# Three of four gated FFNs by Strassen's seven products, on one core

## The chip, the cores and the metric

The kernel runs on one core of one Trainium2 chip. The metric is the device time of one execution in microseconds (us); lower is better. Engines are called TensorE (PE), VectorE (DVE), ScalarE (ACT), GpSimd (POOL) and SyncE (SP, which only issues transfers here).

## What is computed

A trunk of two layers on 520 tokens (512 of a prompt and 8 single ones), model width 1024. Each layer has a gated FFN, a mixer, a second gated FFN and an embedding gate:

```
def swiglu(x, wg, wu, wd):
    return (jax.nn.silu(x @ wg) * (x @ wu)) @ wd
...
x = x + 0.5 * swiglu(rms_norm(x, n_ffn1[i]), w_ffn1_gate[i], w_ffn1_up[i], w_ffn1_down[i])
mix, v, new_buf, hT = hybrid_mix(rms_norm(x, n_mix[i]), ...)
x = x + mix
x = x + 0.5 * swiglu(rms_norm(x, n_ffn2[i]), w_ffn2_gate[i], w_ffn2_up[i], w_ffn2_down[i])
gate = jax.nn.sigmoid(rms_norm(x, n_ple[i]) @ w_ple_gate[i])
x = x + gate * (p @ w_ple_proj[i])
```

The FFN's hidden width is 2816, which is 22 tiles of 128. All data are float32.

## The kernel before

Activations lie feature-major: 128 partitions by 8 feature tiles (XT) by 520 tokens (TOK), and a token row is worked on in two halves of 260 (HALF). Every matrix product is done three times in a rounded format: each operand is cut into a high part (the value rounded to float32r) and a low part (the rest), and the products high by high, high by low and low by high add up in PSUM. So one 128x128 block of weights against 520 tokens is 6 matmuls of 260 columns, and a unit of 8 blocks (one output tile of 1024 inputs) is 48.

Weights come as a stream of units of 512 KB. SP loads unit n into `raw` slot n % 4 once three counts back have been released: it waits for the semaphore `wlo` to reach n - 3. ACT copies `raw` to `w_hi` (L696, function `hi`), DVE subtracts to get `w_lo` (L909, function `lo`, which raises `wlo`). Work is done AHEAD = 3 units ahead. PSUM has two pairs of banks `main` and two `aux`; a unit fills one pair and its reader raises `evac`, and PE waits for the `evac` of two units before.

An FFN runs in three chunks of 8, 8 and 6 hidden tiles. For each tile PE does a gate unit and an up unit. DVE multiplies the gate by the row norms `rstd_b` into `tmp` (L974), ACT applies Silu (L734), DVE scales the up product (L980), multiplies both (L983), ACT cuts the high part of the hidden tile (L739) and DVE the low part (L932, raises `hlo`). Then 8 down units, one for each output tile, use the chunk's hidden tiles: DVE adds half of the product to `x` (L1000). In the third chunk ACT also prepares the next phase's input (L702 high part, L706 square) and DVE its low part (L915); POOL adds the squares (L305, L308), PE sums them over partitions (`stat1`, L472), ACT takes the root (L723) and DVE the reciprocal (L921) that gives `rstd_b`.

Before the second FFN of a layer stand the eight units of the output projection ("OUT"), before the first FFN of the second layer the eight units of the embedding gate ("PG"); behind the second FFN stand four half-size units of the embedding projection ("PP"), behind the first FFN the mixer's units ("XR" first). L673 are the last unit's matmuls, which do one token half after the other.

## Time and profile before

| | |
|---|---|
| median of 3 runs | 1988.18 us (1988.04 to 1988.85) |
| the profiled execution | 1987.9 us, its span 1986.2 us |
| PE busy | 1961.6 us, 16072 matmuls |
| DVE, ACT, POOL busy | 1009.0, 670.9, 137.8 us |
| granted clock of TensorE | 0.997 of full |
| DMA | 190.46 MB, mean 96 GB/s |

The profile's busy times are for the whole span. A matmul's duration overlaps the next one's, so the spacing of matmuls, not the mean duration, gives their price.

### The profile page before, as it was taken

What the parts mean: (1) busy time and instruction counts of PE and PEld (TensorE: products, weight loads), DVE (VectorE), ACT (ScalarE), POOL (GpSimd) and SP (SyncE); (2) the same over time, 40 slices, a digit from 0 to 9 for tenths busy, and PEclk for the clock granted to TensorE, in tenths of its full rate; (3) what the DMA queues carried; (4) which work ended last, traced back from release to release, by engine and by line L of the source; (5) the groups of instructions that cost most, each with busy time, mean ns of one, the idle gap of its engine ahead of it and who ended that gap; (6) DMA issues with size and microseconds to landing.
All of it is one profiled execution on the core that took longest, in us unless ns stands there. A gap on an engine that the chain in (4) does not pass through costs nothing.

```text
span 1986.2 us, 38193 instructions
## 1 busy us (share of the span) xinstructions
PE 1961.6 (99%) x16072; PEld 1942.6 (98%) x16072; DVE 1009.0 (51%) x1216; ACT 670.9 (34%) x848; POOL 137.8 (7%) x181
## 2 busy tenths in 40 slices
PE   7999999999999999999999999999999999999997
PEld 7999999998999999999999999999999999999996
DVE  6444434668554344346854244346775443443465
ACT  5222312445433122124433122124544331221353
POOL 1000000130110000001100000002201000000012
PEclk9999999999999999999999999999999999999998
DMA  5222222322332222223222222222222222222241
GB/s 205 86 97 93 84 96 94 108 84 66 106 119 95 96 85 95 85 95 129 95 85 95 90 91 95 85 95 98 76 94 96 95 91 90 87 94 89 92 139 44
DMA packets 54131, 190.46 MB, mean 96 GB/s; under 512 B 6096, under 2 KB 8432, under 8 KB 54048
## 3 DMA queue, kind: packets, MB, share of 16 engines
q1 hardware_dynamic: 52576, 184.87, 27.6%
q0 software_dynamic: 1472, 4.38, 0.7%
q8 instruction: 65, 1.06, 0.2%
q14 instruction: 18, 0.15, 0.0%
HBM read 186.91 MB, written 2.31 MB: 95 GB/s over the span
## 4 chain that ended last, share of the span: by engine, by line
PE 98%; DVE 1%; ACT 0%; DMA 0%; issue 0%; POOL 0%; DVEq 0%; SPq 0%; ACTq 0%
PE main L447 92%; PE aux L600 2%; PE aux L548 1%; PE aux L447 1%; PE main L504 1%; PE main L600 1%; PE aux L620 0%; PE aux L472 0%; PE main L673 0%; DVE x L1223 0%; DMA raw<-weights_dram 0%; DVE rstd_b L921 0%; DVE rstd_b L1218 0%; PE aux L623 0%; DVE part_lo L915 0%; PE aux L575 0%
## 5 line engine op out<-in xcount | busy, mean ns | idle before, releaser
L447 PE MATMUL main<-part_hi,w_hi 128*128 128x260 f32 x5056 | 1020.9, 283 | 1.9 <-DVE tmp L974 1.5
L447 PE MATMUL main<-part_hi,w_lo 128*128 128x260 f32 x5056 | 1019.4, 283 | 0.0
L447 PE MATMUL main<-part_lo,w_hi 128*128 128x260 f32 x5056 | 1017.2, 283 | 0.0
L447 PEld LDWEIGHTS main<-part_hi,w_hi 128*128 128x128 f32 x5056 | 780.3, 189 | 4.2 <-issue 2.7
L447 PEld LDWEIGHTS main<-part_hi,w_lo 128*128 128x128 f32 x5056 | 779.4, 189 | 0.0
L447 PEld LDWEIGHTS main<-part_lo,w_hi 128*128 128x128 f32 x5056 | 777.0, 188 | 0.0
L909 DVE TENSOR_TENSOR w_lo<-raw,w_hi 128x1024 fp32r<-128x1024 f32 (+1 forms) x344 | 433.2, 1260 | 206.8 <-ACT w_hi L696 195.0
L696 ACT ACTIVATE w_hi<-raw 128x1024 fp32r<-128x1024 f32 (+1 forms) x344 | 355.9, 1038 | 245.4 <-PE main L447 238.8
L739 ACT ACTIVATE part_hi<-tmp 128x520 f32 (+1 forms) x88 | 56.2, 639 | 433.9 <-DVE tmp L983 433.9
L734 ACT ACTIVATE tmp<-tmp 128x520 f32<-128x520 f32 x111 | 71.2, 642 | 357.4 <-DVE tmp L974 324.2
L1000 DVE SCALAR_TENSOR_TENSOR x<-main,x 128x520 f32<-128x520 f32 x96 | 66.8, 696 | 225.4 <-PE main L447 225.4
L980 DVE TENSOR_TENSOR tmp<-main,rstd_b 128x520 f32<-128x520 f32 x88 | 61.5, 699 | 179.1 <-PE main L447 179.1
L974 DVE TENSOR_TENSOR tmp<-main,rstd_b 128x520 f32<-128x520 f32 x87 | 60.8, 699 | 121.1 <-PE main L447 120.4
L305 POOL TENSOR_TENSOR rs<-rs 128x520 f32<-128x520 f32 x8 | 10.7, 1342 | 1468.0 <-ACT rs L706 1468.0
L932 DVE TENSOR_TENSOR part_lo<-tmp,part_hi 128x520 f32 (+1 forms) x88 | 61.7, 701 | 81.9 <-ACT part_hi L739 81.9
L702 ACT ACTIVATE part_hi<-x,vecs 128x520 fp32r<-128x520 f32 x56 | 40.9, 731 | 141.7 <-DVE x L1000 68.8
L308 POOL TENSOR_TENSOR rs<-rs 128x520 f32<-128x520 f32 x47 | 63.4, 1350 | 169.6 <-ACT rs L706 169.6
L915 DVE SCALAR_TENSOR_TENSOR part_lo<-x,vecs,part_hi 128x520 fp32r<-128x520 f32 x64 | 54.4, 855 | 39.7 <-ACT part_hi L702 39.1
L983 DVE TENSOR_TENSOR tmp<-tmp 128x520 f32<-128x520 f32 x88 | 61.7, 701 | 11.3
L706 ACT ACTIVATE rs<-x 128x520 f32<-128x520 f32 x71 | 44.3, 626 | 17.9 <-DVE x L1201 16.2
L921 DVE RECIPROCAL rstd_b<-rstd_b 128x520 f32<-128x520 f32 x8 | 27.2, 3401 | 10.7 <-ACT rstd_b L723 10.7
L734 ACT ACT_TABLE_LOAD x21 | 26.9, 1283 | 0.4
(180 smaller groups left out, 709.9 us busy)
## 6 DMA issues: line engine op xcount, KB each, us to landing
raw<-weights_dram SPq DMA_DIRECT2D x344, 512.0 KB, 3.2
x<-x_in_dram SPq DMA_DIRECT2D x4, 520.0 KB, 7.2
y_out<-x SPq DMA_DIRECT2D x8, 260.0 KB, 2.6
mix<-p_in_dram POOLq DMA_DIRECT2D x2, 520.0 KB, 3.6
ln<-ln_dram POOLq DMA_DIRECT2D x2, 512.0 KB, 3.9
ws<-ws_dram POOLq DMA_DIRECT2D x2, 512.0 KB, 5.7
bs<-bs_dram POOLq DMA_DIRECT2D x2, 256.0 KB, 3.9
bd<-bd_dram POOLq DMA_DIRECT2D x8, 64.0 KB, 6.2
```

The costliest lines, as they stand in the source:

```text
L308: eng.tensor_tensor(rs_sum, rs_sum, sq(n), ALU.add).then_inc(ssum_s, 1)
L447: last = pe.matmul(ps[:, q, 0:HALF], ww[:, s, w], xx[:, k, q * HALF:(q + 1) * HALF], start=(a == 0 and b == 0), stop=(a == kts - 1 and b = ...
L600: last = pe.matmul(vbank[t] if t < NCH else vs, xx[:, k, c:c + P], ww[:, (U_V + u) % SLOTS, kk * WA:(kk + 1) * WA], start=(k == 0 and b == ...
L696: act.activation(w_hi[:, s, 0:c], raw[:, s, 0:c], ACT.Copy).then_inc(whi, 1)
L734: act.activation(dst, src, func).then_inc(f_s, 1)
L739: act.activation(hparts(l)[0][:, bass.ds(k, 1), :], tmp[:, 3:4, :], ACT.Copy).then_inc(hhi, 1)
L909: dve.tensor_tensor(w_lo[:, s, 0:c], raw[:, s, 0:c], w_hi[:, s, 0:c], ALU.subtract).then_inc(wlo, 1)
L932: dve.tensor_tensor(lo_[:, bass.ds(k, 1), :], tmp[:, 3:4, :], hi_[:, bass.ds(k, 1), :], ALU.subtract).then_inc(hlo, 1)
L974: dve.tensor_tensor(halves(T(0)), pair(banks[2 * j]), halves(rstd_b[:, :]), ALU.mult).then_inc(evac, 1)
L980: dve.tensor_tensor(halves(T(2)), pair(banks[2 * j + 1]), halves(rstd_b[:, :]), ALU.mult).then_inc(evac, 1)
L983: dve.tensor_tensor(T(3), T(1), T(2), ALU.mult).then_inc(hf_s, 1)
L1000: dve.scalar_tensor_tensor(halves(x[:, o, :]), pair(main[(par + o) % 2]), 0.5, halves(x[:, o, :]), ALU.mult, ALU.add).then_inc(evac, 1)
```

## The change

The FFNs are changed for all but the first (`seven(l, which)`). The gate and up matrices of one hidden tile are seen as a 2x2 block matrix (gate or up by lower or upper half of the 1024 inputs), the tokens as another (token half by input half). Strassen's scheme in Winograd's form computes the four output quarters from seven products P1 to P7 of half inputs (4 blocks) by half tokens (260), where there were eight. A product is 12 matmuls.

- Four sums of weights for each tile (`tau`, four DVE adds of 512 columns) are cut into high and low (`hi12`, `lo12`, `hi34`, `lo34`), as is the second half of the up unit (`hi_b`, `lo_b`, into `wx`). The gate unit is cut without DVE: ACT writes the rounded value to `w_hi` and the negated rounded value to `w_lo` (`gate_cut`), and a transfer issued by POOL adds the full weights from HBM onto `w_lo`, which leaves the low part there (`gate_low`, 512 KB).
- Four sums of tokens (`sigma`, four DVE operations of 260 columns for each of 4 input tiles, and `sigma_hi`, `sigma_lo`) are made in the last four units before the FFN.
- Partial results share banks: P1 starts bank X and is copied out (`copy_p1`), P6 is added and copied out (`copy_u2`), P7 is added and read by `c22`, P4 is added and read by `c21`. P2 is read by `c11`, P5 and P3 share a bank (`copy_p5`, `c12`).
- The hidden tile's low part is made by ACT writing the negated high part, and a POOL transfer inside SBUF that adds the value (`hidden_low`, 260 KB, from `tmp`).
- Row norms are now applied to each down product in a step of its own before it is added to `x`.
- The loops are written out, and the parameters of layer 2 are loaded later.

The core of the diff (definitions of PE and of the DVE and ACT loops):

```
+                    def P6(t):
+                        pe.wait_ge(lo12_s, S + t + 1)
+                        pe.wait_ge(p1_copy, S + t + 1)
...
+                        product(X(G, t), *slot_w(3, 1), *s2, False, False).then_inc(prod, 1)
...
+                    def P7(t):
+                        pe.wait_ge(u2_copy, S + t + 1)
+                        pe.wait_ge(lo34_s, S + t + 1)
+                        product(X(G, t), *slot_w(2, 0), *s3, False, False).then_inc(prod, 1)
+
+                    def P4(t):
+                        pe.wait_ge(c22_ev, S + t + 1)
+                        product(X(G, t), *slot_w(2, 1), *a22, False, True).then_inc(prod, 1)
...
+                    P1(0)
+                    P1(1)
+                    P2(0)
+                    if first:
+                        stat1(stat)
+                    P2(1)
+                    P6(0)
+                    P5(0)
+                    P7(0)
+                    P4(0)
+                    P6(1)
+                    P5(1)
+                    P3(0)
+                    for g in range(1, tiles - 1):
+                        P1(g + 1)
+                        P7(g)
+                        P2(g + 1)
+                        P4(g)
+                        P6(g + 1)
+                        P5(g + 1)
+                        P3(g)
...
+                    P7(last_t)
...
+                    down_part(0, 0, 2, True)
+                    P4(last_t)
+                    P3(last_t)
+                    down_part(0, 2, tiles, True).then_inc(unit, 1)
...
+            def gate_cut(n, t, T_):
+
+                act.wait_ge(raw_in[n % SLOTS], 16 * (n // SLOTS + 1))
+                act.activation(w_hi[:, gate_slot(t), :], raw[:, n % SLOTS, :], ACT.Copy)
+                act.activation(w_lo[:, gate_slot(t), :], raw[:, n % SLOTS, :], ACT.Copy,
+                               scale=-1.0).then_inc(gate_neg, 1)
...
+            def tau4(n, T_):
+
+                dve.wait_ge(t12, 2 * T_ + 2)
+                dve.wait_ge(gate_neg, T_ + 1)
+                dve.tensor_tensor(tau[:, 3 * HB:4 * HB], tau[:, HB:2 * HB], raw_gate(n, 1), ALU.add).then_inc(wlo, 1)
...
+                    for g in range(1, tiles - 1):
+                        act.wait_ge(unit, n + 2 * g)
+                        hi_b(n + 2 * g, S + g)
+                        copy_p1(g + 1)
+                        h_hi(g - 1)
+                        done(g, "P4")
+                        hi34(n + 2 * g + 2, S + g + 1)
+                        silu(g)
+                        copy_u2(g + 1)
+                        gate(g + 3)
+                        copy_p5(g + 1)
...
+            def sigma_lo(stat, k):
+
+                at = KH * (first_tile(stat // 4, stat % 4 // 2) // HT0) + k
+                hi_, lo_ = xparts(stat // 4)
+                dve.wait_ge(sx_hi, 2 * at + 1)
+                dve.tensor_tensor(sig_all(k, True), sig_raw3, sig_all(k, False), ALU.subtract).then_inc(sx_lo, 1)
...
+                    def c22(t):
+                        done(t, "P7")
+                        dve.wait_ge(p5_copy, S + t + 1)
+                        if S + t >= 2:
+                            dve.wait_ge(h_low[t % 2], 16 * ((S + t) // 2))
+                        dve.tensor_tensor(T(2 + t % 2)[:, A2], X(G, t), p5, ALU.add).then_inc(c22_ev, 1)
...
+                    for g in range(1, tiles - 1):
+                        c12(g - 1)
+                        hidden(g - 1)
+                        lo12(n + 2 * g + 2, S + g + 1)
+                        c22(g)
+                        lo_b(n + 2 * g, S + g)
+                        tau3(n + 2 * g + 2, S + g + 1)
+                        tau4(n + 2 * g + 2, S + g + 1)
+                        c11(g + 1)
+                        c21(g)
+                        c11_r(g + 1)
+                        lo34(n + 2 * g + 2, S + g + 1)
+                        if g + 2 < tiles:
+                            tau1(n + 2 * g + 4, S + g + 2)
+                            tau2(n + 2 * g + 4, S + g + 2)
...
+                        dve.wait_ge(unit, d + j + 1)
+                        dve.tensor_tensor(halves(T(j % 2)), pair(down_bank(G, which, c == 2, j)), halves(rstd_b[:, :]),
+                                          ALU.mult).then_inc(down_ev, 1)
+                        dve.wait_ge(down_ev, XT * (3 * (S // HT0) + c) + j + 1)
+                        dve.scalar_tensor_tensor(x[:, j, :], T(j % 2), 0.5, x[:, j, :],
+                                                 ALU.mult, ALU.add).then_inc(evac, 1)
+                        if c == 2:
+                            x_lo(stat + 1, j)
...
+            def hidden_low(l, which, t0, t):
+
+                T_ = first_tile(l, which) + t0 + t
+                pool.wait_ge(h_neg, T_ + 1)
+                pool.dma_start(hparts(l)[1][:, t, :], T(2 + t % 2), accum_op=ALU.add).then_inc(h_low[t % 2], 16)
```

How the instructions now stand, at three places. First DVE in the middle of a chunk, before: one hidden tile (`raw` and `w_hi` are weights, `tmp` products, `part_lo` the hidden tile's low part).

```order
L974 TENSOR_TENSOR tmp<-main,rstd_b 128x520 [waits unit]
...
L909 TENSOR_TENSOR w_lo<-raw,w_hi 128x1024 [waits whi]
L980 TENSOR_TENSOR tmp<-main,rstd_b 128x520 [waits unit]
...
L983 TENSOR_TENSOR tmp<-tmp 128x520 [waits f_s]
...
L932 TENSOR_TENSOR part_lo<-tmp,part_hi 128x520
...
L909 TENSOR_TENSOR w_lo<-raw,w_hi 128x1024 [waits whi]
```

The same place now, from `c12` to `lo34` (two adds for the tile after, `tau1` and `tau2`, follow):

```order
L1569 TENSOR_TENSOR tmp<-aux,mix 128x260 [waits unit]
L1574 SCALAR_TENSOR_TENSOR tmp<-tmp 128x520 [waits f_s,evac]
L1508 TENSOR_TENSOR w_lo<-tau,w_hi 128x1024 [waits whi]
L1565 TENSOR_TENSOR tmp<-main,mix 128x260 [waits h_low1,p5_copy,prod]
L1518 TENSOR_TENSOR wx<-raw,wx 128x512 [waits hib_s]
L1497 TENSOR_TENSOR tau<-raw 128x512 [waits lo34_s]
L1503 TENSOR_TENSOR tau<-tau,raw 128x512 [waits gate_neg,t12]
L1550 TENSOR_TENSOR tmp<-main,mix 128x260 [waits hf_s,p1_copy,prod]
L1558 TENSOR_TENSOR tmp<-main,rstd_b 128x260 [waits prod]
L1554 TENSOR_TENSOR tmp<-tmp,rstd_b 128x260 [waits c11_ev]
L1513 TENSOR_TENSOR w_lo<-tau,w_hi 128x1024 [waits hi34_s]
```

The read of P7's bank (`c22`, L1565), for which PE's P4 waits, now stands behind a weight cut (`lo12`, L1508), and the add that releases the gate's `raw` slot (`tau4`, L1503) stands four places behind that cut.

Second, ACT in the same loop, where before there was one hidden tile's Silu, high part and two weight copies:

```order
L1059 ACTIVATE wx<-raw 128x512 [waits raw_in3,unit]
L1117 ACTIVATE mix<-main 128x260 [waits c11_ev,prod]
L1144 ACTIVATE part_hi<-tmp 128x520 [waits hf_s]
L1145 ACTIVATE part_lo<-tmp 128x520
L1054 ACTIVATE w_hi<-tau 128x1024 [waits wlo,prod]
L1140 ACTIVATE tmp<-tmp 128x520 [waits c21_ev]
L1123 ACTIVATE mix<-main 128x260 [waits evac,prod]
L1042 ACTIVATE w_hi<-raw 128x1024 [waits raw_in0,prod]
L1043 ACTIVATE w_lo<-raw 128x1024
L1129 ACTIVATE mix<-aux 128x260 [waits c22_ev,prod]
L1049 ACTIVATE w_hi<-tau 128x1024 [waits t12]
```

The gate's two copies (`gate_cut`, L1042 and L1043), which wait for a load, stand ahead of `copy_p5` (L1129) and `hi12` (L1049), and so ahead of what DVE's `lo12` waits for.

Third, DVE in the third chunk's down units, before:

```order
L1000 SCALAR_TENSOR_TENSOR x<-main,x 128x520 [waits unit]
L915 SCALAR_TENSOR_TENSOR part_lo<-x,vecs,part_hi 128x520 [waits xhi]
L909 TENSOR_TENSOR w_lo<-raw,w_hi 128x1024 [waits whi]
L1000 SCALAR_TENSOR_TENSOR x<-main,x 128x520 [waits unit]
L915 SCALAR_TENSOR_TENSOR part_lo<-x,vecs,part_hi 128x520 [waits xhi]
```

and now:

```order
L1632 TENSOR_TENSOR tmp<-main,rstd_b 128x520 [waits unit]
L1635 SCALAR_TENSOR_TENSOR x<-tmp,x 128x520 [waits down_ev]
L1395 SCALAR_TENSOR_TENSOR part_lo<-x,vecs,part_hi 128x520 [waits xhi]
L1389 TENSOR_TENSOR w_lo<-raw,w_hi 128x1024 [waits whi]
L1632 TENSOR_TENSOR tmp<-main,rstd_b 128x520 [waits unit]
```

One operation of 520 columns and a wait for its result have come into each unit's step.

## Rows read from the trace of the kernel before

**Rows 1.** The page: span, busy time and share of each engine, chain by engine
```profile
span 1986.2 us, 38193 instructions
PE 1961.6 (99%) x16072; PEld 1942.6 (98%) x16072; DVE 1009.0 (51%) x1216; ACT 670.9 (34%) x848; POOL 137.8 (7%) x181
PE 98%; DVE 1%; ACT 0%; DMA 0%; issue 0%; POOL 0%; DVEq 0%; SPq 0%; ACTq 0%
```

**Rows 2.** The chain that ended last, longest pieces: start, us, what
```profile
557.06 374.58 PE main L447 x3120
...
1964.01 5.77 PE main L673 x48
```

**Rows 3.** Stretches: us, busy time of each engine, granted clock, DMA, GB/s
```profile
550.00:925.00 375.00, 375.00 (x3122) 374.88 (x3121) 167.26 (x185) 107.41 (x129) 12.98 (x15) 1.00 0.29 97
```

**Rows 4.** Groups by shape: busy us, mean ns of one, idle before it
```profile
L909 DVE TENSOR_TENSOR w_lo<-raw,w_hi 128x1024 fp32r<-128x1024 f32 x336 | 423.4, 1261 | 205.1 <-ACT w_hi L696 193.2 <-PE aux L447 0.9
L447 PE MATMUL main<-part_hi,w_hi 128*128 128x260 f32 x5056 | 1020.9, 283 | 1.9 <-DVE tmp L974 1.5 <-DVE part_lo L915 0.3
L921 DVE RECIPROCAL rstd_b<-rstd_b 128x520 f32<-128x520 f32 x8 | 27.2, 3401 | 10.7 <-ACT rstd_b L723 10.7
L1085 DVE TENSOR_TENSOR tmp<-rstd_b,ident 128x512 f32<-128x512 f32 x2 | 1.4, 684 | 0.0
L1210 DVE TENSOR_TENSOR tmp<-main,rstd_b 128x260 f32<-128x260 f32 x2 | 0.9, 430 | 0.2
L739 ACT ACTIVATE part_hi<-tmp 128x520 f32 x86 | 55.0, 639 | 430.4 <-DVE tmp L983 430.4
L728 ACT ACTIVATE rstd_b<-aux,small 128x260 f32<-128x260 f32 x2 | 0.9, 468 | 0.2 <-PE aux L682 0.2
```

**Rows 5.** One hand-over from ACT over DVE to SP, in order of time
```profile
61.08 1.04 ACT L696 ACTIVATE w_hi<-raw 128x1024 fp32r<-128x1024 f32 x1
62.16 1.23 DVE L909 TENSOR_TENSOR w_lo<-raw,w_hi 128x1024 fp32r<-128x1024 f32 x1
63.56 0.33 SPq L326 DMA_DIRECT2D raw<-weights_dram  x1
```

**Rows 6.** ACT, two weight copies in a row
```profile
109.74 2.17 ACT L696 ACTIVATE w_hi<-raw 128x1024 fp32r<-128x1024 f32 x2
```

**Rows 7.** Transfers: KB each, median us to landing; spread of L326; shares
```profile
raw<-weights_dram SPq DMA_DIRECT2D x344, 512.0 KB, 3.2
DMA to landing us min/median/max: 3.0/3.2/8.4
mix<-p_in_dram POOLq DMA_DIRECT2D x2, 520.0 KB, 3.6
ws<-ws_dram POOLq DMA_DIRECT2D x2, 512.0 KB, 5.7
q1 hardware_dynamic: 52576, 184.87, 27.6%
```

**Rows 8.** The chain: hand-over from PE to ACT, then from DVE to PE
```profile
24.67 0.02 issue
...
29.64 0.14 issue
```

**Rows 9.** DVE and POOL in the third chunk's down units
```profile
914.80 0.69 DVE L1000 SCALAR_TENSOR_TENSOR x<-main,x 128x520 f32<-128x520 f32 x1
916.29 0.76 DVE L915 SCALAR_TENSOR_TENSOR part_lo<-x,vecs,part_hi 128x520 fp32r<-128x520 f32 x1 [0.80 <-ACT part_hi L702]
917.77 1.54 DVE L909 TENSOR_TENSOR w_lo<-raw,w_hi 128x1024 fp32r<-128x1024 f32 x1 [0.72 <-ACT w_hi L696]
919.23 0.68 DVE L1000 SCALAR_TENSOR_TENSOR x<-main,x 128x520 f32<-128x520 f32 x1
```

**Rows 10.** DVE and POOL in the last units of PG
```profile
985.10 1.31 POOL L308 TENSOR_TENSOR rs<-rs 128x520 f32<-128x520 f32 x1 [4.45 <-ACT rs L706]
985.18 1.79 DVE L915 SCALAR_TENSOR_TENSOR part_lo<-x,vecs,part_hi 128x520 fp32r<-128x520 f32 x1
```

More of the change, by code:

```diff
@@ L112, with seven, first_tile, products @@
 THIRD = 2
+def seven(l, which):
+    return (l, which) != (0, 0)
+def first_tile(l, which):
+    return HT0 * sum(seven(a, b) for a in range(DEPTH) for b in range(2) if (a, b) < (l, which))
+KH = XT // 2
+HB = KH * P
+def products(tiles, t, name):
+    if t == 0:
+        return {"P1": 1, "P2": 3, "P6": 5, "P5": 6, "P7": 7, "P4": 8}[name]
+    if t == 1 and name in ("P1", "P2", "P6", "P5"):
+        return {"P1": 2, "P2": 4, "P6": 9, "P5": 10}[name]
+    if name in ("P1", "P2", "P6", "P5"):
+        return 10 + 6 * (t - 2) + {"P1": 1, "P2": 3, "P6": 5, "P5": 6}[name]
+    if t == tiles - 1:
+        return 6 * tiles - 2 + {"P7": 1, "P4": 2}[name]
+    return 10 + 6 * (t - 1) + {"P7": 2, "P4": 4}[name]
 def main_slot(g):
@@ L474, in stat1, with product @@
                 last.then_inc(st1, 1)
+            def product(ps, hi_w, lo_w, hi_x, lo_x, start, stop, k_wait=None):
+                for k in range(KH):
+                    if k_wait is not None:
+                        k_wait(k)
+                    w = slice(k * P, (k + 1) * P)
+                    for b, (ww, xx) in enumerate(((hi_w, hi_x), (hi_w, lo_x), (lo_w, hi_x))):
+                        last = pe.matmul(ps, ww[:, w], xx(k), start=(start and k == 0 and b == 0),
+                                         stop=(stop and k == KH - 1 and b == 2), skip_group_check=True)
+                return last
@@ L476, in ffn @@
             def ffn(l, which, u0, g0):
+                if seven(l, which):
+                    return seven_ffn(l, which, u0, g0)
                 stat = 4 * l + 2 * which
@@ L741, in ffn @@
             def ffn(l, which, u0, g0):
+                if seven(l, which):
+                    return seven_ffn(l, which, u0, g0)
                 stat = 4 * l + 2 * which
@@ new lines, in lo12, with lo34, lo_b @@
+            def lo12(n, T_):
+                dve.wait_ge(whi, n + 2)
+                dve.tensor_tensor(w_lo[:, 3, :], tau12, w_hi[:, 3, :], ALU.subtract).then_inc(lo12_s, 1)
+            def lo34(n, T_):
+                dve.wait_ge(hi34_s, T_ + 1)
+                dve.tensor_tensor(w_lo[:, 2, :], tau34, w_hi[:, 2, :], ALU.subtract).then_inc(lo34_s, 1)
+            def lo_b(n, T_, units=1):
+                dve.wait_ge(hib_s, T_ + 1)
+                dve.tensor_tensor(wx_lo, raw_up(n, 1), wx_hi, ALU.subtract).then_inc(wlo, units)
@@ L965, in ffn @@
             def ffn(l, which, u0, g0):
+                if seven(l, which):
+                    return seven_ffn(l, which, u0, g0)
                 stat = 4 * l + 2 * which
@@ L1041, in _ @@
             lo(0, 0)
+            dve.tensor_scalar(ngain[:, :], vecs[:, V_G:V_GF], -1.0, None, ALU.mult).then_inc(ng_s, 1)
+            dve.wait_ge(ng_s, 1)
             for o in range(XT):
```

517 lines of the change are left out of this document (484 added, 33 removed).

## The prediction

> **What bounds the kernel now.** I read the page's busy times and its chain first [rows 1]: PE is busy 99% of the span and is 98% of the chain that ended last. The chain in order of time shows PE running alone for whole FFNs [rows 2]: 374.58 us for 3120 matmuls, 0.1201 us each, at full clock [rows 3]. So only what shortens PE's matmuls, or makes PE wait, counts. DVE (51%) and ACT (34%) have room on average [rows 1], but they idle behind PE's units (the last column of [rows 4]), and the question is whether what they now owe PE within one hidden tile comes in time.
>
> **What the change removes.** A hidden tile takes 84 matmuls for 96. With 22 tiles and three FFNs that is 792 fewer, 792 x 0.1201 = 95.1 us. A product does one token half with high-high, high-low, low-high weights in turn and adds into one bank all the time; the last unit (L673) does exactly that, 48 in 5.77 us, 0.1202 each [rows 2]. So the price of a matmul stays. A product is 1.44 us, a tile's seven 10.09 us (11.53 before).
>
> **What it adds: prices.** DVE: 1024 columns 1.23 to 1.26, 520 0.70, 512 0.68, 260 0.43, the reciprocal 3.40 us [rows 4, 5]. ACT: 1024 1.04, two in a row 2.17, 520 0.64, 260 0.41 to 0.47 [rows 4 to 6]. Hand-overs: ACT to DVE 0.04, DVE to SP's issue 0.17 [rows 5], DVE to PE 0.14 [rows 8], PE to a reader 0.2 (0.02 [rows 8] and the last matmul, 0.28 long at a spacing of 0.12 [rows 4]); a load lands 3.2 us after issue [rows 7]. DVE operations that are ready follow each other without a gap or overlap by 0.08 (L909 to L1000 [rows 9]); one that needs the result before it waits 0.12.
>
> DVE's work for a tile is two cuts of 1024 (2.5), five operations of 512 (3.4), five of 260 (2.1) and one of 520 (0.7): 8.7 of 10.09 us. ACT's is four of 1024, one of 512, three of 520 and three of 260, about 8. They fit as sums, but not as chains:
>
> *The loop over a tile.* `tau4` of tile g+1 releases the gate's `raw` slot; SP issues the load of the gate of tile g+3, ACT waits for it with `gate_cut`, and behind that in its queue stand `copy_p5` and `hi12`; DVE's `lo12` waits for `hi12`, and behind it stand `c22`, `lo_b`, `tau3` and the next `tau4`. Round: 0.17 + 3.2 + 0.1 + 2.17 + 0.33 + 0.94 + 0.04 + 1.23 + 0.35 + 0.61 + 0.61 + 0.61 = 10.35 us, for PE's 10.09. PE waits at P4, which needs `c22`. In the prologue P4 of tile 0 waits 0.8 us (P7 done, 0.2 + 0.43 + 0.14, with nothing between), `tau4` of tile 1 is done 2.2 us after P4 starts, and the first `c22` of the loop lies 0.8 us late; each further round adds 0.26. A chunk of 8 has 5 such rounds, one of 6 has 3 (at the end `gate_cut` is one copy, and the round 1.1 us shorter): 1.8 + 1.8 + 1.3 = 5 us for each FFN, 15 for three. But the 3.2 us are of loads that hardly meet another: DMA is busy 28% [rows 7]. Now the load of the up unit (issued 1.3 us before), the 260 KB of `hidden_low` and this load come within 3 us. At 184.87 MB in 27.6% of the span [rows 1, 7] 512 KB need 1.6 us of all DMA engines, so a meeting costs between 0 and 1.6 us. I take 0.4: with 13 rounds in each FFN, 39 in all, 15.6 more. **Loop: 30.6 us** (15 to 77).
>
> *Joints at the start of chunks two and three.* P4's 0.8 and the second bank: the down product's reading is now two operations (0.2 + 0.70 + 0.12 + 0.70 + 0.14 = 1.86 us against 1.44 of P1), 0.44. Six joints: **7.4**.
>
> *The first down unit of a chunk.* After P3 of the last tile: 0.2, `c12` 0.43, 0.12, `hidden` 0.70, then on ACT two of 520 (1.3 with the hand-over), then POOL's transfer, then PE. Without the transfer 2.85 + 0.14 us. Its landing no row shows: a plain POOL transfer of 520 KB takes 3.6, a queued one 5.7 [rows 7]; I take 4.2, nearer to the plain one. PE has 5 blocks of 0.72 us to do first in a chunk of 8 and 3 in one of 6, so it waits 3.6, 3.6 and 5.0: **36.6** for three FFNs (31 to 50). Before, DVE's subtraction gave the low part within 0.9 us of the high one, under the same cover.
>
> *The third chunk's down units.* Before, a DVE step took 919.23 - 914.80 = 4.43 us [rows 9] beside PE's 36 x 0.1201 = 4.32. Now it has 0.70 + 0.12 more, 5.24. The last input tile's low part is done 39.7 us after the first unit, and PE, at 30.2 + 5.05 for its last block, waits 4.6; behind the second FFNs the smaller PP units need the weights of steps 5 to 7 and wait 5.1. **14.7** for three (10 to 18).
>
> *The first chunk's start.* In OUT, steps with `sigma`, `sigma_lo` and `tau` take 5.7, 6.8, 5.4 and 7.2 us for units of 5.77; then `sigma_lo` of the last tile stands behind `lo12` and P6(0) needs it (4 us late), then `lo_b`, `tau1`, `tau2`, `c11`, the reciprocal 3.4, `c11_r` and `c22` stand one behind the other, 7.2 us where PE has 4.3: 7 us. In PG a step also has the gate's three operations (8.2, 6.8, 7.3): 12 us. Before, the reciprocal was hidden under two free bank pairs. 7 + 7 + 12 = **26** (15 to 35).
>
> Parameter loads, ACT's extra table load, written-out loops and POOL's issues (137.8 us busy [rows 1]) cost nothing: PE's units and POOL's idle time hide them; uncovered, POOL's issues alone would be 0.6 us on a round.
>
> Sum: 30.6 + 7.4 + 36.6 + 14.7 + 26 = 115.3, less 95.1, is +20.2 us. The profiled execution took 1987.9 us, the median of the runs is 1988.18, the same within 0.02%. **2008 us.**
>
> **A rule against the change.** DVE's L915 takes 1.79 us when a POOL add of squares starts beside it [rows 10] and 0.76 otherwise [rows 9]. The Trainium skill (SBUF — State Buffer, Who interferes with whom) has it that a VectorE instruction with two SBUF inputs and a GpSimd instruction that reads SBUF exclude each other; the trace agrees. The new starts have some three more such meetings each, about 9 us in all, which would make the sum 2017; I leave them in the range. The skill (Collectives: The Full Stack, The bandwidth ceiling) also says that a transfer that adds reads two sources and so costs twice on the read side; no row here shows one. By it `hidden_low` would land like a transfer of double size, an estimate within the bounds above.
>
> **The rivals.**
> 1. *The loop does not bind* (faster). The round is 10.35 against 10.09; a round that is 0.3 us shorter with loads at their usual 3.2 makes it vanish, and the starts then shrink with the same shorter hand-overs. Loop 0 to 3, start 20, joints 7, first down units 31, third chunk 13: 73, so 1966. For it: 3.0 us loads exist [rows 7], ready operations overlap. Against: three transfers now meet. It decides once loop and starts together are under 30 us. Chance 0.22; up to 1984.
> 2. *The waits just eat the gain* (1984 to 1992). All transfers at their lower bounds: 15 + 7.4 + 31 + 14.7 + 26 = 94, so 1987. Chance 0.13.
> 3. *The adding transfers are slow*: landing 5.7 us, and the raw loads beside them 0.9 us later. First down units +13.5, loop +0.5 x 39 = 19.5: 2041; if `gate_low` passed the 8.8 us that lie between `gate_cut`'s end and P1 of that tile (two PE rounds less ACT's place in them), each round would grow by the excess and it would be 2060 and more. For it: the queued row of 5.7. Against: bandwidth is there, 28%. Chance 0.20.
> 4. *Matmuls don't get cheaper* (a product slower than 12 x 0.120): the change doesn't do what it says. Against it L673. Chance 0.02, over 2060.
>
> **How the numbers follow.** A run of this kernel can be told from another at about 0.2%, 4 us. The forecast, slower by 1992 to 2030, has 0.43. Faster 0.22, within 0.2% 0.13, slower 0.43 + 0.20 + 0.02 = 0.65. The range leaves out half of the first rival and the far end of the third: 1970 to 2050; the likeliest case's own range is 1994 to 2028.
>
> **What the profile after would show.** PE 15280 matmuls at 0.120 us; between P7 and P4 gaps of 0.7 to 1 us per tile, ended by `c22` (right), or none (rival 1); ACT idle before L1042 ended by the load; PE idle of 3 to 5 us at L754 nine times, ended by POOL's or the DMA's `h_low`; `w_lo` transfers landing in 4 to 6 us; PE waits at the next phase's first unit for L1395. I am wrong if PE's idle total is far from 130 us, above all if ACT does not wait for `raw`.

## The result, and the profile after

| | before | after |
|---|---|---|
| median (runs) | 1988.31 us (1988.04 to 1988.85, 4) | 2108.81 us (2104.93 to 2111.95, 4) |
| ratio | | 1.0605, 95% interval 1.0586 to 1.0623 |
| profiled span | 1986.2 us | 2103.2 us |
| PE busy, idle | 1961.6, 24.6 us | 1938.9, 164.3 us |

The change makes the kernel slower by 6%, 101 us beyond the forecast of 2008. It takes away the matmuls as forecast: 15280 for 16072. The page of the changed kernel, to be read against [rows 1]:

```profile
span 2103.2 us, 37548 instructions
...
PE 1938.9 (92%) x15280; PEld 1899.5 (90%) x15280; DVE 1279.6 (61%) x1823; ACT 929.1 (44%) x1337; POOL 255.6 (12%) x313
...
PE 56%; DMA 15%; DVE 12%; ACT 9%; issue 6%; POOL 0%; DVEq 0%; SPq 0%; ACTq 0%; POOLq 0%
```

PE was 98% of the chain and is 56% of it; DMA, DVE, ACT and issue have the rest. The next view, what PE waited for (us in total, times, longest), says where:

```profile
PE main L650 <- DVE tmp L1565: 78.8, 59, 3.8
PE aux L754 <- DMA part_lo<-tmp: 33.1, 13, 5.1
PE main L650 <- DMA w_lo<-weights_dram: 13.8, 3, 4.9
PE main L810 <- DVE part_lo L1395: 8.4, 1, 8.4
PE main L650 <- DVE tmp L1406: 5.4, 1, 5.4
PE main L614 <- DVE x L1635: 3.6, 2, 1.9
```

The first row is P4 waiting for `c22`, the second the first down unit of a chunk waiting for `hidden_low`, the third and fifth the starts of the three FFNs. L810 is the kernel's own start, which the kernel before has as well. The transfers of after, against [rows 7]:

```profile
q1 hardware_dynamic: 52576, 184.87, 26.8%
q0 software_dynamic: 20480, 56.56, 15.2%
...
raw<-weights_dram SPq DMA_DIRECT2D x344, 512.0 KB, 3.5
w_lo<-weights_dram POOLq DMA_DIRECT2D x66, 512.0 KB, 5.4
part_lo<-tmp POOLq DMA_DIRECT2D x66, 260.0 KB, 5.9
```

The median over all raw loads, 3.5 us, hides the loops: of the 14 raw loads issued between 584 and 660 us, in the first loop of an FFN, landing takes at least, in the median and at most

```profile
DMA to landing us min/median/max: 3.4/5.4/6.7
```

Two rounds of that loop in the chain that ended last (start, us, what):

```profile
597.51 6.70 DMA raw<-weights_dram
...
604.62 0.63 issue
605.25 1.04 ACT w_lo L1043
...
606.57 0.94 ACT w_hi L1049
607.51 0.52 ACT wx L1059
...
608.69 0.42 DVE tmp L1565
609.11 0.60 DVE wx L1518
609.70 0.60 DVE tau L1497
610.31 0.61 DVE tau L1503
...
611.08 5.53 DMA raw<-weights_dram
...
623.49 5.55 DMA raw<-weights_dram
```

This is the cycle that the prediction laid out, load, gate's cut (L1042, L1043), `hi12` (L1049), DVE's queue with `c22` (L1565), `lo_b`, `tau3`, `tau4` (L1503), next load. (Between 607.5 and 608.7 us the chain names ACT's next operation, L1059; on DVE `lo12`, L1508, runs from 607.54 to 608.77 us, and `c22` follows it, as forecast.) Its loads start at 597.51, 611.08, 623.49 and 635.93 us: a round of 12.4 to 13.6 us for PE's 10.09.

One number holds for all these rounds. The round less the landing of its load is 13.57 - 6.70 = 6.87, 12.41 - 5.53 = 6.88 and 12.44 - 5.55 = 6.89 us. So a round is its load's landing plus 6.9 us, and each microsecond of landing above 3.2 makes it longer than PE's work by as much.

### The profile page after: what moved, and what is told of

Read it like the earlier page. It is cut to its first block, busy times and chain, and to the rows that moved or that the text cites. A ratio compares the mean times of both kernels' runs of the same rounds, so it can differ in the third digit from the quotient of the medians.

```text
span 2103.2 us, 37548 instructions
## 1 busy us (share of the span) xinstructions
PE 1938.9 (92%) x15280; PEld 1899.5 (90%) x15280; DVE 1279.6 (61%) x1823; ACT 929.1 (44%) x1337; POOL 255.6 (12%) x313
## 3 DMA queue, kind: packets, MB, share of 16 engines
q0 software_dynamic: 20480, 56.56, 15.2%
## 4 chain that ended last, share of the span: by engine, by line
PE 56%; DMA 15%; DVE 12%; ACT 9%; issue 6%; POOL 0%; DVEq 0%; SPq 0%; ACTq 0%; POOLq 0%
PE main L614 30%; DMA raw<-weights_dram 12%; PE main L754 11%; PE main L650 5%; PE aux L754 3%; DMA part_lo<-tmp 3%; PE aux L906 2%; ACT w_hi L1049 2%; ACT w_lo L1043 2%; PE aux L650 2%; DVE w_lo L1389 2%; DVE wx L1518 1%; ACT wx L1059 1%; DVE tau L1497 1%; DVE tau L1503 1%
## 5 line engine op out<-in xcount | busy, mean ns | idle before, releaser
L614 PE MATMUL main<-part_hi,w_hi 128*128 128x260 f32 x1888 | 382.4, 284 | 3.5 <-DVE tmp L1656 1.5
L614 PE MATMUL main<-part_hi,w_lo 128*128 128x260 f32 x1888 | 380.1, 283 | 0.0
L614 PE MATMUL main<-part_lo,w_hi 128*128 128x260 f32 x1888 | 379.3, 282 | 0.0
L650 PE MATMUL main<-part_hi,w_hi 128*128 128x260 f32 x792 | 241.6, 305 | 98.7 <-DVE tmp L1565 78.8
L1389 DVE TENSOR_TENSOR w_lo<-raw,w_hi 128x1024 fp32r<-128x1024 f32 (+1 forms) x194 | 245.8, 1269 | 104.2 <-ACT w_hi L1002 100.6
L614 PEld LDWEIGHTS main<-part_hi,w_hi 128*128 128x128 f32 x1888 | 291.6, 188 | 5.8 <-issue 3.5
L614 PEld LDWEIGHTS main<-part_hi,w_lo 128*128 128x128 f32 x1888 | 290.6, 188 | 0.0
L614 PEld LDWEIGHTS main<-part_lo,w_hi 128*128 128x128 f32 x1888 | 290.1, 188 | 0.0
L650 PEld LDWEIGHTS main<-part_hi,w_hi 128*128 128x128 f32 x792 | 157.2, 198 | 113.8 <-DVE tmp L1565 92.0
L650 PE MATMUL main<-part_lo,w_hi 128*128 128x260 f32 x792 | 233.1, 294 | 0.0
L650 PE MATMUL main<-part_hi,w_lo 128*128 128x260 f32 x792 | 233.1, 294 | 0.0
L650 PE MATMUL main<-sig,w_hi 128*128 128x260 f32 x1056 | 205.2, 291 | 0.0
L650 PEld LDWEIGHTS main<-sig,w_hi 128*128 128x128 f32 x1056 | 171.5, 198 | 0.0
L754 PE MATMUL main<-part_hi,w_hi 128*128 128x260 f32 x816 | 167.5, 287 | 1.5 <-DVE x L1635 1.5
L754 PE MATMUL main<-part_lo,w_hi 128*128 128x260 f32 x816 | 166.3, 286 | 0.0
L754 PE MATMUL main<-part_hi,w_lo 128*128 128x260 f32 x816 | 166.2, 286 | 0.0
L650 PEld LDWEIGHTS main<-part_hi,w_lo 128*128 128x128 f32 x792 | 158.9, 201 | 0.0
L650 PEld LDWEIGHTS main<-part_lo,w_hi 128*128 128x128 f32 x792 | 158.8, 200 | 0.1
L1508 DVE TENSOR_TENSOR w_lo<-tau,w_hi 128x1024 fp32r<-128x1024 f32 x66 | 80.7, 1223 | 127.0 <-ACT w_hi L1049 127.0
L650 PE MATMUL main<-sig,w_lo 128*128 128x260 f32 x528 | 153.2, 290 | 0.0
L1042 ACT ACTIVATE w_hi<-raw 128x1024 fp32r<-128x1024 f32 x66 | 69.9, 1060 | 176.6 <-DMA raw<-weights_dram 102.8
```

Of the source, the lines that this page charges most:

```text
L614: last = pe.matmul(ps[:, q, 0:HALF], ww[:, s, w], xx[:, k, q * HALF:(q + 1) * HALF], start=(a == 0 and b == 0), stop=(a == kts - 1 and b = ...
L650: last = pe.matmul(ps, ww[:, w], xx(k), start=(start and k == 0 and b == 0), stop=(stop and k == KH - 1 and b == 2), skip_group_check=True)
L754: last = pe.matmul(ps[:, q, 0:HALF], ww[:, j % SLOTS, w], xx[:, k, q * HALF:(q + 1) * HALF], start=(k == 0 and b == 0), stop=(k == tiles - ...
L1042: act.activation(w_hi[:, gate_slot(t), :], raw[:, n % SLOTS, :], ACT.Copy)
L1389: dve.tensor_tensor(w_lo[:, s, 0:c], raw[:, s, 0:c], w_hi[:, s, 0:c], ALU.subtract).then_inc(wlo, 1)
L1508: dve.tensor_tensor(w_lo[:, 3, :], tau12, w_hi[:, 3, :], ALU.subtract).then_inc(lo12_s, 1)
```

## The experiments

Seventeen kernels. Six take the price of the transfers apart; the rest are on the clock and on the order of the queues. All times are medians, each compared with runs of the kernel before on its own chip (1988.2 to 1988.6 us, so the chips differ by 0.02%). The runs with a small or a plain transfer compute something else than the kernel; only their times are of use. Code is abridged: `...` and the ends of some lines are left out.

### 1. Who makes the load late

The first run cuts both adding transfers to 16 columns.

```
-  pool.dma_start(w_lo[:, gate_slot(t), :], weights[n, :, :], accum_op=ALU.add)
+  pool.dma_start(w_lo[:, gate_slot(t), 0:16], weights[n, :, 0:16], accum_op=ALU.add)
-  pool.dma_start(hparts(l)[1][:, t, :], T(2 + t % 2), accum_op=ALU.add)
+  pool.dma_start(hparts(l)[1][:, t, 0:16], T(2 + t % 2)[:, 0:16], accum_op=ALU.add)
```

> Both adding transfers of POOL (the gate's low part, 512 KB, and the hidden tile's, 260 KB) move only 16 of their columns; all else, their issue, their semaphores and every wait, stays. The rest of the low parts then holds the negated high part, so the output differs. Theory A (the adding transfers take DMA from the raw weight loads and land late themselves): the raw load in the loop lands in about 3.3 us instead of 5.5, a round falls from 12.5 to about 10.4 us, 39 rounds give 80 us, the nine first down units 30, the three starts 10, and TensorE's granted clock in the loop goes back to 1.00: 1985 us (1970 to 2005). Rival B (the load is late because the two raw loads of a round meet each other, and the rest of the loop is DVE's and ACT's own chain): only the down units and the starts gain, 2065 us (2055 to 2080), and the raw load stays above 5 us.

Measured 2011.56 us, 97 less than the changed kernel. Theory A had 124, rival B 44: neither. The loads in the loop (median of the same stretch) land in 4.3 us, not in 3.3.

The two transfers apart:

> Only the hidden tile's adding transfer (260 KB inside SBUF) moves 16 of its columns; the low part's other columns hold the negated high part. Theory A: the nine first down units give 30 us, and the round gets a part of its 2 us back (this transfer is issued 1.4 us ahead of the gate's raw load), some 1 us x 39: 2040 us (2020 to 2060). Rival B: the down units alone, 2078 us (2070 to 2085).

> Only the gate's adding transfer (512 KB from HBM) moves 16 of its columns; the gate's low part otherwise holds the negated high part. Theory A: the three starts give 10 us and the rounds some 1 us x 39, as this transfer runs in the other half of the round: 2055 us (2035 to 2080). Rival B: the starts alone, 2098 us (2090 to 2105).

Measured 2021.3 us with the hidden tile's transfer small (the lower end of Theory A's range) and 2099.7 with the gate's (rival B's number, 2098). So 87.5 us hang on the transfer of 260 KB and 9.1 on the one of 512 KB; Theory A was wrong to share them out evenly. Alone the 9.1 us are little more than the noise (1.0566, 1.0538 to 1.0594, against 1.0605, 1.0586 to 1.0623), but the first run gives each price again: 9.7 us for the gate's transfer with the hidden tile's small, 88.1 for the hidden tile's with the gate's small. The two add up to the 97.

Size doesn't set the price. With both small, q0 takes 2.4% of the engines' time, with the gate's kept 11.9%, with the hidden tile's kept 6.1%: the costlier transfer by the engines' time is the cheap one. The likely reason is when each is issued. The gate's (606.59 us in the rounds above) starts 4.5 us ahead of the load that bounds the round and lands in 5.4, and PE's P1 wants it two rounds later; the hidden tile's starts at 609.65, 1.4 us ahead of that load. No run moved either in time, and the two differ also in where they read from (HBM or SBUF), so this is argued, not shown. The two views of the run with the small hidden transfer, landing of raw loads in the same stretch and PE's waits:

```profile
DMA to landing us min/median/max: 3.3/4.4/5.3
```

```profile
PE main L651 <- DVE tmp L1566: 46.7, 49, 2.5
PE aux L755 <- DMA part_lo<-tmp: 14.8, 11, 3.1
```

P4's waits fall by 32.1 us, the first down units' by 18.3; PE's busy time falls by 33.5 us as well, with the same matmuls (1905.4 for 1938.9). The rounds in its chain are again the landing plus 6.9 us: 608.93 to 620.31 us, less 4.51, is 6.87.

Is it the adding, or that there is a third transfer?

```
-  pool.dma_start(hparts(l)[1][:, t, :], T(2 + t % 2), accum_op=ALU.add)
+  pool.dma_start(hparts(l)[1][:, t, :], T(2 + t % 2))
```

> Both transfers keep their size, queue and waits but copy instead of adding, so the low parts hold the whole values. If the price lies in the adding (the reading of a second source), Theory A': landings of 5.4 and 5.9 us fall to about 3.6, the round by 1 us: 2050 us (2030 to 2075). If any third transfer costs the same, Theory A'': 2105 us (2095 to 2112).

> The changed kernel with the hidden tile's transfer as a plain copy of the same 260 KB inside SBUF instead of an adding one (the low part then holds the whole value); the gate's transfer still adds. If the adding is the price: most of the 61 us that both plain transfers gave, 2055 us (2045 to 2070), and the raw load in the loop at 4.6. If the presence of the transfer is the price: 2100 us.

Measured 2047.95 us with both plain and 2056.26 with the hidden tile's alone plain, both as forecast if the adding is the price. 52.5 of the 87.5 us are the price of adding, 35 that of the transfer's presence. The transfers and the raw loads in the run with the hidden tile's plain:

```profile
part_lo<-tmp POOLq DMA_DIRECT2D x66, 260.0 KB, 4.6
```

```profile
DMA to landing us min/median/max: 3.2/4.7/6.8
```

4.6 us for 5.9, and 0.7 us off the raw load. Some of the 1.3 us lies ahead of the data: POOL takes 0.88 us to issue the adding transfer and 0.55 to issue the plain one.

What is left of the load's delay without the hidden transfer, 4.4 us against 3.2, was tested by cutting every second raw load too:

```
+                    c = 16 if s % 2 else UNIT
-                    sp.dma_start(raw[:, s, :]...
+                    sp.dma_start(raw[:, s, 0:c]...
```

> The run with the hidden tile's transfer cut to 16 columns (2021 us), in which also every second load of raw weights (the odd units, in the FFNs the up units) moves 16 columns only, so that the gate's load meets no other weight load; the rest of these weights is what an earlier load left. If the two raw loads of a round meet each other (rival B's mechanism for the last 1.2 us): the gate's load lands in 3.3 us, the P4 gaps shrink by 1 us each, 2000 us (1990 to 2010). If not: 2021 us and a landing of 4.4.

Measured 1988.13 us, 33 less than with the hidden transfer cut alone, and 12 below the forecast of 2000. (The cut takes the odd units of the whole kernel, not the up units alone, but PE's waits for `c22` make up 30.7 of the 33 us: 46.7 to 16.0.) In its chain the gate's loads, and rounds of 10.5 us:

```profile
605.38 3.63 DMA raw<-weights_dram
...
615.89 3.77 DMA raw<-weights_dram
```

So rival B's mechanism is real too: the up unit's load, issued 1.2 us ahead, delays the gate's without any adding. Between 560 and 960 us the loads of the chain's steady rounds land in 3.4 to 3.9 us here and in 4.5 to 4.9 with the up unit's load whole, 0.9 us or so more, and 39 rounds of that are about the 33 us. Both causes sit in the same 5.5 us.

### 2. The clock

In after, PE comes out of a gap at the lower clock level. The rows of PE at P4 (start, us, engine, line, operation, idle before it):

```profile
609.16 0.58 PE L650 MATMUL main<-part_hi,w_hi 128*128 128x260 f32 x1 [3.22 <-DVE tmp L1565]
...
609.76 0.42 PE L650 MATMUL main<-part_hi,w_lo 128*128 128x260 f32 x1
```

Starts lie 0.22 us apart where they lay 0.12 before, for the 27 matmuls up to 615.15 us; then they are 0.12 again. The granted clock is 1.00 in nearly all of the kernel before [rows 3], and in after's loops

```profile
584.00:660.00 76.00, 67.01 (x527) 65.97 (x526) 49.11 (x80) 39.83 (x64) 9.06 (x11) 0.96 0.61 149
...
706.00:806.00 100.00, 90.85 (x712) 89.00 (x711) 65.49 (x104) 53.91 (x86) 11.44 (x14) 0.97 0.55 136
```

The columns are the stretch, its length, the busy time of PE, its weight loads, DVE, ACT and POOL, the granted clock, DMA's share and GB/s. PE's busy time is 72.4 us above 1961.6 - 95.1. The prediction had no such term, so this looked like most of the missing 101 us. The test fills the gaps with matmuls whose result nobody reads:

```
                     def P4(t):
+                        if 0 < t < tiles - 1:
+                            for k in range(12):
+                                pe.matmul(aux[1][:, 0, 0:HALF], slot_w(2, 0)[0][:, 0:P], a22[0](0), ...)
                         pe.wait_ge(c22_ev, S + t + 1)
```

> The changed kernel with 12 extra matmuls (1.44 us at full clock) issued ahead of P4's wait in each of the 39 + 9 - 9 loop rounds, into a bank that nobody reads then; they add work and no result uses them. In the changed kernel P4's first matmul follows an idle gap of up to 3.8 us (59 gaps, 78.8 us) and PE then runs at 0.21 us a matmul for a while. Theory F (the gaps also cost clock, and the slow matmuls lie on the path): the fillers shorten the gaps, the granted clock in the first FFN2 loop goes from 0.96 to 1.00, PE's busy time per matmul back to 0.122, and the kernel gets faster in spite of 468 more matmuls: 2085 us (2070 to 2100). Theory G (the round's chain goes through the raw load, so PE's slow matmuls are hidden behind it): the clock rises and the time stays, 2108 us within 6. Theory H (the fillers simply delay P4): 2125 us or more.

(The edit reaches 48 rounds and 576 matmuls; the expectation counted them as 39 and 468.) Measured 2109.56 us, no change (1.0621 for 1.0605). PE's waits for `c22`, and three loads of the chain:

```profile
PE main L650 <- DVE tmp L1569: 35.6, 34, 2.3
```

```profile
597.50 5.90 DMA raw<-weights_dram
...
610.28 7.20 DMA raw<-weights_dram
...
624.36 6.06 DMA raw<-weights_dram
```

The clock in the first loop went from 0.96 to 1.00, the gaps from 78.8 to 35.6 us, and the time stayed: Theory G. The unchanged time alone could be a gain and a loss that cancel, as a filler of 1.44 us is longer than many a gap. The rounds rule that out for the loops: they are 12.78 and 14.08 us here, less the landing 6.88 and 6.88, the same 6.9 as with PE at the lower level. In the loops the slow matmuls cost nothing, because the chain runs through the load, beside PE. They are a mark of the gaps, not a cause.

### 3. Getting the load out of the cycle

The gate's cut behind the short operations in ACT's queue:

```
                         copy_u2(g + 1)
-                        gate(g + 3)
                         copy_p5(g + 1)
                         if g + 2 < tiles:
                             hi12(n + 2 * g + 4, S + g + 2)
+                        gate(g + 3)
```

> The changed kernel with ACT's queue reordered alone: in each round the gate's cut, which waits for the raw load, stands behind the copy of P5 and the high part of the first two combined weights. Theory C (the load bounds the round because the short operations stand behind it in ACT's queue): the load of 5.5 us leaves the chain, the chunks with 8 tiles lose most of their P4 gaps: 2055 us (2035 to 2075), the first down units unchanged. Rival D (the load only moves on, to the high part of the up half and the copy of P1, which now stand behind it): 2105 us or slower.

Measured 2084.29 us: 24.5 less, between C and D. The rows of its chain show D's mechanism, with another load than I had named:

```profile
608.96 0.70 DVE wx L1518
...
609.68 0.05 SPq L447
...
609.82 5.70 DMA raw<-weights_dram
...
615.59 0.70 DVE tau L1485
```

Now `lo_b` releases the up slot, and the up load, which `tau1` waits for, closes a cycle of its own through `hi12` and the gate's cut. And `gate_low` comes late: PE's wait for it is 32.0 us in 20 waits, where it was 13.8 in 3.

The hidden tile's low part on DVE, as before the change:

```
-    act.activation(hparts(l)[1][:, t, :], T(2 + t % 2), ACT.Copy, scale=-1.0)
-    (POOL's transfer hidden_low)
+    dve.tensor_tensor(hparts(l)[1][:, t, :], T(2 + t % 2), hparts(l)[0][:, t, :], ALU.subtract)
```

> The changed kernel with the hidden tile's adding transfer replaced by a subtraction on DVE, as in the kernel before (one DVE operation of 520 columns more for each tile, one ACT copy less, no transfer). The run with this transfer cut to 16 columns took 2021 us, with 8 KB still landing 3.8 us after issue. Theory A: this one also saves that landing at the nine first down units (9 x 3 = 27 us) and pays at most 0.7 us x 39 on DVE's part of the round: 2005 us (1990 to 2025). Rival E (DVE's extra operations lengthen the round's chain more than the transfer did): over 2035 us.

Measured 2005.16 us, as Theory A. With one DVE operation of 0.70 us a tile in the transfer's place, 104 us go.

> Both edits of the two runs above together: low half of the hidden tile on DVE, and the gate's cut behind the copy of P5 and the combined weights' high part. If both theories A and C hold, the round is PE's own 10.1 us and only starts, joints and the third chunk's down units stay: 1975 us (1960 to 1995), faster than before. If the gate's cut only moves the wait on (D): as the run with DVE's subtraction alone.

> The kernel with both edits, and in each round DVE's sum for C22, which PE's P4 waits for, ahead of the 1.23 us low part of the combined weights (which P6 needs 1.44 us later). If DVE's queue order sets the gap at P4: 1.2 us less for a gap where one is, 15 to 30 us below the run with both edits. If P4's gap is ended by P7's end and the copy: no change from it (within 4 us).

Measured 2013.22 and 2010.34 us: the ACT order that gave 24.5 us with the late loads costs 8 us here, and `c22` first changes nothing beyond noise (2.9 us). PE's waits for `gate_low` rise from 15.7 us in 3 waits to 24.9 in 13, and with `c22` first the waits for `c22` fall (37.7 to 12.9 us) while those for `gate_low` (32.6) and for the copy of P1 (16.3) rise. The wait moves on and the time stays.

An order that releases the gate's slot before DVE waits for ACT:

```
-                        lo12(n + 2 * g + 2, S + g + 1)
-                        c22(g)
                         lo_b(n + 2 * g, S + g)
+                        c22(g)
                         tau3(n + 2 * g + 2, S + g + 1)
                         tau4(n + 2 * g + 2, S + g + 1)
+                        lo12(n + 2 * g + 2, S + g + 1)
```

and on ACT `copy_p5` ahead of the gate's cut.

> The run with the hidden tile's low half on DVE (2005 us), and an order that takes the load out of the round's chain: on DVE, low part of the up half, C22, the last two combined weights (which release the raw slot), and only then the 1.23 us low part that waits for ACT; on ACT the copy of P5 ahead of the gate's cut, which waits for the load. Theory I (the remaining P4 gaps, 45.9 us, and the half-level clock behind them, about 35 us, come from the cycle load, cut, high part, low part, release): the gate's load is issued some 3 us earlier in the round, the gaps go, clock 1.00 in the loops: 1950 us (1935 to 1970). Rival J (DVE is now late itself, at 9.4 of 10.1 us a round): 1985 to 2005 us, with PE waiting at P6 for the low part instead of at P4.

> The same order on DVE and ACT, with the hidden tile's adding transfer kept. Theory I: the later landing of the load (5.4 us) has slack now, so the loops are PE's own and only the nine first down units (36 us) and the starts stay: 1985 us (1970 to 2005). Rival J: the order moves the wait to P6, 2060 us or more.

Measured 1993.17 us (1.0025, 1.0015 to 1.0035) and 2127.2 us. The same order gains 12 us with DVE's subtraction and loses 18 with the transfer, where the raw load takes 6.2 us in the median (7.06, 7.36 and 7.14 in three rounds of the chain). The order did shorten its part: the round less the landing is 6.0 us in both runs, for 6.9. But the landing grew by more with the transfer, which is now issued 0.8 us ahead of the load, and 6.0 + 7.1 us is a longer round than 6.9 + 5.5. Theory I was wrong for both by 40 us and more, rival J right for the first; for the second its time holds (2060 or more), but the wait that it named is the smaller one (22.1 us at P6 beside 68.5 at P4).

P2(0) ahead of P1(1) at the start of chunks, since P1(1) waits for its `gate_low`; and the same with matmuls in the gaps:

> The same without the extra matmuls: only the order of the first four products. P2(0) has its operands when P1(1) still waits for its low part (4.9 us at three starts), so 1.4 us of each such gap is filled with work: 1989 us (1985 to 1992). If DVE's queue binds the starts, 1993 us, no change.

> The version with the new order and DVE's subtraction (1993 us), with PE's first four products in the order P1(0), P2(0), P1(1), P2(1) at each chunk's start, and at each FFN's start 24 extra matmuls ahead of P1(1)'s wait for its low part and 12 ahead of P4(0)'s wait for the reciprocal, whose result nobody reads. In the version without them PE's 24 matmuls after the 4.9 us gap take 5.4 us at the lower clock level instead of 2.9, and the ones after the next gap 4.6 instead of 2.9, and here PE stands on the chain. Theory F' (the half level costs time where PE is on the path): 3 x (1.4 for the order + 2.5 + 1.7) = 17 us less, 1977 us (1970 to 1984), faster than before. Rival K (the starts hang on DVE's queue, so faster matmuls only wait longer): within 4 us of the run with the order alone.

Measured 1990.3 us (1.0009, 1.0000 to 1.0018) and 2004.21 us. The swap gave 2.9 us, hardly more than the noise; P2(0) now waits for DVE's low part of the last input tile (10.3 us in 3 waits). The fillers cost 13.9 us, which neither theory had, and the chain shows where:

```profile
556.96 0.68 DVE part_lo L1455
...
557.68 1.02 PE main L646 x3
558.70 4.72 PE aux L680 x24
563.42 1.46 PE main L646 x12
```

L680 is the fillers' line. They came behind P2(0)'s wait instead of into it, and ran at the lower level themselves: 4.72, 4.84 and 5.00 us at the three starts, 14.6 us on the chain. So whether a filler in the right place would pay at a start was not tested.

Last, two orders within the round:

> The version with DVE's subtraction, the new order and P2(0) ahead of P1(1) (1990 us); in each round DVE's low part of the first two combined weights, which P6 waits 0.5 us for, goes ahead of the last combined weight, which releases the gate's raw slot. If only DVE's queue sets P6: 19 us less, 1972 us. If the load (landing 5 us) has no slack: the load is 1.2 us later each round, the gain is lost, 1990 to 2015 us.

> The same version; in each round the third combined weight (0.6 us on DVE, nothing to wait for) goes into the 1.5 us in which DVE idles ahead of the low part of the up half. Release of the raw slot and the low part that P6 waits for both come 0.6 us earlier: the P6 gaps (19.3 us) go and the round is 10.3 us: 1970 us (1965 to 1980), faster than before. If the round hangs on the load and on ACT's queue behind it alone: 0.6 us x 39 less at most for the chain, but not for PE's wait at P4: 1980 us.

Measured 2012.85 us and 1987.2 us (0.9999, 0.9990 to 1.0008). In the first, PE's waits for `lo12` fall from 19.3 to 4.8 us and those for `c22` rise from 11.0 to 40.3: the load, released 1.2 us later, has no slack to give. In the second, `tau3` in DVE's idle stretch takes the waits for `lo12` to 5.2 us, but those for `c22` grow to 17.1, and 3 us of the forecast 20 come, no more than noise. PE's waits in it:

```profile
PE main L646 <- DVE tmp L1558: 17.1, 27, 2.5
PE main L646 <- DVE part_lo L1445: 10.9, 3, 3.7
...
PE main L646 <- DVE w_lo L1503: 5.2, 9, 0.6
```

This is the fastest version of the change that was run, and it can't be told from the kernel before.

What the orders did shows when each round is split into the landing of the gate's load and the rest (us, rounds of the chain between 560 and 960 us that run from one gate's load to the next by the cycle above):

| kernel | the rest | landing | round |
|---|---|---|---|
| changed kernel | 6.9 | 3.9 to 6.7 | 10.8 to 13.6 |
| with fillers | 6.9 | 5.5 to 7.2 | 12.4 to 14.1 |
| hidden transfer small | 6.9 | 4.5 to 4.9 | 11.4 to 11.8 |
| DVE's subtraction | 6.9 | 4.3 to 4.8 | 11.2 to 11.7 |
| DVE's subtraction and the new order | 6.0 | 4.7 to 5.2 | 10.7 to 11.2 |
| new order with the transfer | 6.0 | 6.7 to 8.6 | 12.7 to 14.6 |
| `lo12` ahead of `tau4` | 7.1 | 4.3 to 4.9 | 11.4 to 12.0 |
| `tau3` first | 5.4 | 5.2 to 5.7 | 10.6 to 11.1 |

The rest is fixed by the order to some 0.02 us. The landing isn't: with DVE's subtraction it grows as the order releases the slot sooner. The gate's adding transfer, 5.4 us long, is issued 4.5 us ahead of the load in the first such version, 3.6 in the new order and 3.0 with `tau3` first, so it is in flight for longer beside it. That would explain the growth; no run separates it from the up unit's load, which moves as well.

## Why the prediction was wrong

- **The saving** of 95.1 us, right: 15280 matmuls, and where nothing disturbs them 288 take 34.60 us, 0.1201 each. Rival 4 is out.
- **The loop**, the right cycle and the wrong size; here the prediction failed. The step was: "a meeting costs between 0 and 1.6 us. I take 0.4". The loads in the loop take 5.4 us in the median, 2.2 over their 3.2, and 5.5 to 6.7 in the rounds shown, so even the upper bound was too low, and a round is 12.4 to 13.6 us for the forecast 10.75. All of it is the landing: the other terms of the round sum to 7.15 in the prediction and measure 6.9. The bound came from the mean share of the DMA engines for a plain load, and it counted the adding transfer by its KB. By the runs the hidden transfer costs 87.5 us (52.5 for adding, 35 for being there; 18 of the whole at the first down units), the gate's 9.1, and the raw loads' meeting each other another 33 once the hidden transfer is small. The prediction had a part of these costs in its 15.6 us for meetings and its landing of 4.2, so they are not a division of the 101 us above the forecast.
- **Joints**: forecast 7.4; the row of `c22` holds them together with the loop, 78.8 us of waits for 38, with slow matmuls behind some of the waits. Not told apart.
- **First down unit**: forecast 36.6, PE's wait 33.1 us. The landing was taken as 4.2 and is 5.9, 7.58 in one second-FFN chunk (922.32 us). There the prediction's own terms give a wait of 2.99 + 7.58 - 2.16 = 8.4 us, and PE waited 5.09: what PE had to do meanwhile was taken too short. The sum was right by luck, by two errors, and it left out the slow matmuls behind these waits (below).
- **Third chunk's down units**: forecast 14.7 from a DVE step of 5.24 us. The step is 5.15 (`L1632` at 938.70, 943.94 and 949.09 us in the chain, 5.24 and 5.15), but PE's idle for it is 5.7 us (3.6 + 1.5 + 0.6), ended by L1635 and not by L1395 as forecast (1.4 us). PE comes late into these units: behind the wait for `hidden_low` its first 48 matmuls take 8.73 us (2.97 + 5.76 in the chain from 929.95 us) for 5.77, at a granted clock of 0.69 from 929 to 940 us and 1.00 after. That this shortens the later waits is argued, not shown.
- **Starts**: forecast 26; the rows have 13.8 + 5.4, and 2.3 and 2.5 at P4 for two of the three starts, some 26 with the third. Right in size, wrong in place: I had counted DVE's queue alone, and the first wait is the landing of the second tile's `gate_low`. Its chain:

```profile
549.71 0.54 ACT rs L1030
...
550.33 1.31 POOL rs L429
551.63 0.79 issue
552.44 5.19 DMA w_lo<-weights_dram
...
557.76 5.54 PE main L650 x24
```

(The chain names POOL's add; what released the transfer is ACT's cut L1043, done at 552.14 us, for which POOL sat idle.)

- **Left out**: the granted clock. It costs nothing in the loops (run with fillers). At the starts PE stands on the chain and 24 matmuls take 5.54 us for 2.9 (last row above), so about 2.6 us at each of three starts. PE stands on the chain behind the nine waits for `hidden_low` too; 12 matmuls take 2.95 to 3.01 us for 1.44 behind five of them (929.95, 1293.89, 1414.90, 1724.10 and 1990.63 us). From the spacing of PE's rows behind all nine I estimate 12 us. So the term is some 20 us; no run tests it.
- **The rule against the change** held: `sigma`'s first operation takes 1.58 us when POOL's add starts beside it, 0.48 otherwise,

```profile
550.34 1.58 DVE L1459 SCALAR_TENSOR_TENSOR tmp<-x,vecs,tmp 128x260 f32<-128x260 f32 x1
551.84 0.48 DVE L1461 SCALAR_TENSOR_TENSOR tmp<-x,vecs,tmp 128x260 f32<-128x260 f32 x1
```

as the Trainium skill has it (SBUF — State Buffer, Who interferes with whom). The other rule of the Trainium skill (Collectives: The Full Stack, The bandwidth ceiling), stated there for the adding step of a collective, that the add needs two source reads and so twice the traffic on the read side, now has a row: 56.56 MB take 15.2% of the DMA engines' time with adding and 9.1% without, 1.7 times (of spans of 2103 and 2043 us). That is in line with it; the row is of reads and writes together.
- **The rivals**: rival 3 was the one that came, a landing of 5.7 us (5.9 measured) and raw loads later by 0.9 us (2.2 measured, against 3.2). I had given it 0.20 and priced it at 2041. Rivals 1 and 2 fell with the load. I had named PE's idle total as what would show me wrong. It is 164 us, 140 above the kernel before's where 115 were forecast, so it shows 24 of the missed 101 us. Most of the rest stands in PE's busy time, as matmuls at the lower level count as busy.

## What to carry to other kernels

A transfer is not free because its engines are a quarter busy: ask which load is in flight when it is issued, and whether that load stands in a cycle with the compute queues. Here an adding transfer of 260 KB issued 1.4 us ahead of the load that bounds the loop cost ten times as much as one of 512 KB issued at another point (that the point is the reason is argued), and an instruction of 0.70 us on an engine with room replaced it. Split the round of such a cycle into the landing of its load and the rest. The rest was the same to 0.02 us in all such rounds of one order (7.1, 6.9, 6.0 and 5.4 us for four orders), and the prediction had it within 0.3; the landing it had not, and with DVE's subtraction that grew under the orders that released the load sooner.
